# Ring of five weight slots with in-place low parts, and the order of silu, cast, product and split

## The reference

```python
def first_block(x, ...):
    proj = rmsnorm(h, norm1_w) @ w_in
    o_d = diff_attention(...)            # 8 heads, two softmax maps each
    o_c = chunk_attention(...)           # 8 heads
    merged = sigmoid(gd) * (o_d @ w_branch_diff) + sigmoid(gc) * (o_c @ w_branch_chunk)
    h = h + merged @ w_out
    h = h + peer(rmsnorm(h, norm2_w), wq, keys, u, v)   # top 16 of 128 x 128 keys, gelu(x u) * g, @ v
    return rmsnorm(h, final_norm_w)

def swiglu(x, w_gu, w_down):
    gate, up = split(x @ w_gu, 2)        # 1024 -> 2 x 2816
    return (silu(gate) * up) @ w_down

def second_block(x, ...):
    x = x + 0.5 * rms_norm(swiglu(rms_norm(x, ffn1_pre_g), ffn1_w_gu, ffn1_w_down), ffn1_post_g)
    x = x + rms_norm(hybrid_mixer(rms_norm(x, mix_pre_g), ...), mix_post_g)
    x = x + 0.5 * rms_norm(swiglu(rms_norm(x, ffn2_pre_g), ffn2_w_gu, ffn2_w_down), ffn2_post_g)
    return x
```

## Time and profile before

| | us |
|---|---|
| median of 3 runs | 1537.48 |
| lowest and highest run | 1533.52, 1541.29 |
| the profiled execution | 1530.73 |
| its span, first to last instruction | 1529.2 |
| PE busy with matmuls | 1495.4 (98%) |
| DVE busy | 1114.7 (73%) |
| ACT busy | 738.3 (48%) |
| POOL busy | 267.9 (18%) |

### The profile page before, as it was taken

One profiled execution on the slowest core, in us unless ns is written; L12 is line 12 of the kernel. 1 busy time (PEld: TensorE's weight loads), 2 busy tenths in 40 slices (PEclk: granted clock), 3 DMA queues, 4 the chain that ended last, 5 costly groups with the idle time before them and its releaser, 6 DMA issues. The chain is left out here.

```text
span 1529.2 us, 27764 instructions
## 1 busy us (share of the span) xinstructions
PE 1495.4 (98%) x10806; PEld 1378.3 (90%) x10806; DVE 1114.7 (73%) x1579; ACT 738.3 (48%) x850; POOL 267.9 (18%) x306
## 2 busy tenths in 40 slices
PE   8999999999999999999999999999899999999998
PEld 7888998999999999998888888889899888899986
DVE  5657666699999989837676777677677576777753
ACT  4366753545454455444444444445344457644431
POOL 1100000000000111025565456540000010000000
PEclk9999999999999999999999999999999999999999
DMA  6553343666665777797877778774556543255551
GB/s 250 211 193 139 118 150 105 214 245 237 235 235 207 255 234 272 259 325 286 288 287 280 298 289 299 285 257 152 190 197 212 195 143 127 97 190 196 193 200 74
DMA packets 56535, 329.47 MB, mean 215 GB/s; under 512 B 7520, under 2 KB 7568, under 8 KB 25088
## 3 DMA queue, kind: packets, MB, share of 16 engines
q1 hardware_dynamic: 36144, 259.01, 47.0%
q0 software_dynamic: 20304, 69.21, 13.1%
HBM read 294.64 MB, written 33.55 MB: 215 GB/s over the span
## 5 line engine op out<-in xcount | busy, mean ns | idle before, releaser
L954 DVE TENSOR_TENSOR wl<-raw,wh 128x2048 fp32r<-128x2048 f32 x244 | 586.9, 2406 | 257.0 <-ACT wh L552 255.8
L552 ACT CAST wh<-raw 128x2048 fp32r<-128x2048 f32 x244 | 466.2, 1911 | 400.6 <-DMA raw<-in_wstream 333.0
L1878 PE MATMUL ub<-xh,wh 128*128 128x256 f32 x2168 | 613.1, 283 | 12.7 <-DVE fg L1069 7.2
L1879 PE MATMUL ub<-xl,wh 128*128 128x256 f32 x2168 | 604.8, 279 | 0.0
L1880 PE MATMUL ub<-xh,wl 128*128 128x256 f32 x2168 | 604.8, 279 | 0.0
L1878 PEld LDWEIGHTS ub<-xh,wh 128*128 128x128 f32 x2168 | 411.5, 190 | 21.9 <-DVE fg L1069 7.8
L1879 PEld LDWEIGHTS ub<-xl,wh 128*128 128x128 f32 x2168 | 412.8, 190 | 0.1
L1880 PEld LDWEIGHTS ub<-xh,wl 128*128 128x128 f32 x2168 | 411.3, 190 | 0.0
L1878 PE MATMUL acc<-wh,ah 128*128 128x512 f32 x512 | 200.0, 391 | 0.2
L1880 PE MATMUL acc<-wh,al 128*128 128x512 f32 x512 | 199.2, 389 | 0.0
L1879 PE MATMUL acc<-wl,ah 128*128 128x512 f32 x512 | 199.2, 389 | 0.0
(11 more groups left out here) (373 smaller groups left out, 1667.4 us busy)
## 6 DMA issues: line engine op xcount, KB each, us to landing
raw<-in_wstream SPq DMA_DIRECT2D x244, 1024.0 KB, 4.9
gates<-gst POOLq DMA_DIRECT2D x16, 1024.0 KB, 15.5
gl_in<-gates POOLq DMA_DIRECT2D x64, 256.0 KB, 4.9
hidden<-hid POOLq DMA_DIRECT2D x60, 256.0 KB, 4.5
hid<-hidden POOLq DMA_DIRECT2D x60, 256.0 KB, 4.8
resid<-in_x SPq DMA_DIRECT2D x2, 512.0 KB, 3.9
raw<-in_wstream SPq DMA_DIRECT2D x2, 512.0 KB, 7.2
rb<-in_rel POOLq DMA_DIRECT2D x1, 1024.0 KB, 8.7
```

The lines of the kernel that those rows point to most:

```text
L552: act.copy(wh[:, slot, :], raw[:, slot % RAW, :]).then_inc(w_high, 1)
L954: v.tensor_tensor(wl[:, slot, :], raw[:, slot % RAW, :], wh[:, slot, :].bitcast(F32), ALU.subtract).then_inc(w_low, 1)
L1878: pe.matmul(dst, sh, mh, start=first, stop=False)
L1879: pe.matmul(dst, sh, ml, start=False, stop=False)
```

## The change

- The ring has five slots. `raw` has five as well, and it is laid in the same bytes as `wl`: a chunk lands where its low part will stand, and DVE subtracts in place. `wh` grows from four to five slots; the total of the three is what it was (80 KB per partition).
- SP loads chunk c when PE is finished with chunk c-5 (`c_done`). Five chunks are loaded at the start in place of two. ACT's cast waits for the landing alone.
- `AHEAD` stays 3.
- Loops over four chunks no longer fit a ring of five. Those of the hidden stage and of the feed-forward stages are written out; those of the value stage on ACT, DVE and PE have a body of 20 chunks (`VBODY`).
- In the feed-forward stages ACT runs the silu of a unit in front of the cast, for the written-out units as silu 0, `ahead(C + 1)`, silu 1, `ahead(C + 2)` and so on, and a silu of one column is put in front of the first one. From unit 6 on DVE runs take and finish in front of the low part. Between units 5 and 6 both engines thus have one conversion fewer, and each later one stands one unit later than before.

```diff
-RAW = 2
-RING = 4
-AHEAD = RING - 1
+RING = 5
+AHEAD = 3
+VBODY = 4 * RING
...
-        raw = sb("raw", [P, RAW, CW])
         wh = sb("wh", [P, RING, CW], F32R)
+        st = ExitStack()
+        raw = sb("raw", [P, RING, CW], at=st)
+        st.close()
         wl = sb("wl", [P, RING, CW], F32R)
...
-            sp.dma_start(raw[:, 1, :], stream[1]).then_inc(raw_in[1], 16)
-
-            def load(c, slot):
-                sp.wait_ge(w_low, c - RAW + 1)
-                sp.dma_start(raw[:, slot, :],
-                             stream[bass.ds(c, 1)].rearrange("a p n -> p (a n)")).then_inc(raw_in[slot], 16)
...
+            for c in range(1, RING):
+                sp.dma_start(raw[:, c, :], stream[c]).then_inc(raw_in[c], 16)
+
+            with sp.Fori(0, NCH // RING - 1) as i:
+                for j in range(RING):
+                    sp.wait_ge(c_done, i * RING + (j + 1))
+                    sp.dma_start(raw[:, j, :], stream[bass.ds(i * RING + (RING + j), 1)]
+                                 .rearrange("a p n -> p (a n)")).then_inc(raw_in[j], 16)
...
-                act.wait_ge(raw_in[slot % RAW], arrived(c, slot))
-                if not isinstance(c, int) or c >= RING:
-                    act.wait_ge(c_done, c - RING + 1)
-                act.copy(wh[:, slot, :], raw[:, slot % RAW, :]).then_inc(w_high, 1)
+                slot = c % RING
+                act.wait_ge(raw_in[slot], c // RING * 16 + 16)
+                act.copy(wh[:, slot, :], raw[:, slot, :]).then_inc(w_high, 1)
...
-            with act.Fori((TOPK_U + SPREAD_U) // 4, 15) as i:
-                for j in range(4):
-                    hidden_step(i * 4 + j, j)
+            for n in range(TOPK_U + SPREAD_U, 60):
+                hidden_step(n, n)
...
-            with act.Fori(0, 15) as i:
-                for j in range(4):
-                    value_step(i, j)
+            with act.Fori(0, 60 // VBODY) as i:
+                for j in range(VBODY):
+                    high_step(i * VBODY + (j + 1), j + 1)
+                    ahead_in(i, CV + j)
...
                 ahead(C)
-                ahead(C + 1)
+
+                act.activation(ssq[:, 7:8], wcol[:, 0, 0:1], ACT.Silu)
                 for j in range(6):
                     silu(U + j, nf + j, j % 2)
-                    if j >= 1 and j < 5:
+                    if j < 5:
                         ahead(C + j + 1)
-                with act.Fori(1, 5) as i:
-                    for j in range(2, 6):
-                        ahead_at(i * 4 + (C + j), C + j)
-                        silu(i * 4 + (U + j), i * 4 + (nf + j), j % 2)
+                for j in range(6, FT):
+                    silu(U + j, nf + j, j % 2)
+                    ahead(C + j)
...
-                v.tensor_tensor(wl[:, slot, :], raw[:, slot % RAW, :], wh[:, slot, :].bitcast(F32),
+                v.tensor_tensor(wl[:, slot, :], raw[:, slot, :], wh[:, slot, :].bitcast(F32),
                                 ALU.subtract).then_inc(w_low, 1)
...
-                with v.Fori(1, 5) as i:
-                    for j in range(2, 6):
-                        ahead_at(i * 4 + (C + j), C + j)
-                        take(i * 4 + (C + j), (U + j) % 2, j % 2)
-                        finish(i * 4 + (U + j), i * 4 + (nf + j), j % 2, bass.ds(i * 4 + j, 1))
+                for j in range(6, FT):
+                    take(C + j, (U + j) % 2, j % 2)
+                    finish_first(j)
+                    ahead(C + j)
...
-            with pe.Fori((TOPK_U + SPREAD_U) // 4, 16) as i:
-                for j in range(4):
-                    hidden_step(i * 4 + j, j)
+            for n in range(TOPK_U + SPREAD_U, 64):
+                hidden_step(n, n)
...
-            with pe.Fori(1, 15) as i:
-                for j in range(4):
+            with pe.Fori(1, 60 // VBODY) as i:
+                for j in range(VBODY):
                     value_step(i, j)
...
-                with pe.Fori(1, 5) as i:
-                    for j in range(2, 6):
-                        unit_chunk(i * 4 + (C + j), C + j, i * 4 + (U + j), U + j)
+                for j in range(6, FT):
+                    unit_chunk(C + j, C + j, U + j, U + j)
```

More of the change, by code:

```diff
@@ L265, in in_bank @@
             return k + 1 if k < 2 else (k | 1) + 1
-        raw_in = [sem(f"raw_in{k}") for k in range(RAW)]
+        raw_in = [sem(f"raw_in{k}") for k in range(RING)]
         first_in = sem("first_in")
@@ L546, in _, with split, ahead_in @@
         def _(act):
-            def split(c, slot):
-                act.wait_ge(raw_in[slot % RAW], arrived(c, slot))
-                if not isinstance(c, int) or c >= RING:
-                    act.wait_ge(c_done, c - RING + 1)
-                act.copy(wh[:, slot, :], raw[:, slot % RAW, :]).then_inc(w_high, 1)
-            def arrived(c, slot):
-                return ((c - slot % RAW) // RAW) * 16 + 16 if isinstance(c, int) else \
-                    (c - slot % RAW) * (16 // RAW) + 16
-            def ahead(c):
[L561 to L565, removed]
+            def split(c):
+                slot = c % RING
+                act.wait_ge(raw_in[slot], c // RING * 16 + 16)
+                act.copy(wh[:, slot, :], raw[:, slot, :]).then_inc(w_high, 1)
+            def ahead(c):
+                if c + AHEAD < NCH:
+                    split(c + AHEAD)
+            def ahead_in(i, c):
+                c += AHEAD
+                slot = c % RING
+                act.wait_ge(raw_in[slot], i * (VBODY // RING * 16) + (c // RING * 16 + 16))
+                act.copy(wh[:, slot, :], raw[:, slot, :]).then_inc(w_high, 1)
             nt = [0]
@@ L741, in hidden_step @@
             def hidden_step(n, nmod):
-                ahead_at(n + CU, CU + nmod)
+                ahead(n + CU)
                 act.wait_ge(c_done, n + (CU + 1))
@@ L791, in _ @@
                 hidden_step(n, n)
[L793 to L797, removed]
-            with act.Fori(0, 15) as i:
-                for j in range(4):
-                    value_step(i, j)
-            for j in range(4):
-                value_step(15, j)
+            with act.Fori(0, 60 // VBODY) as i:
+                for j in range(VBODY):
+                    high_step(i * VBODY + (j + 1), j + 1)
+                    ahead_in(i, CV + j)
+            for n in range(60, 64):
+                if n < 63:
+                    high_step(n + 1, n + 1)
+                    ahead(n + CV)
             def ffn(gu, dn, nf, w, stage):
@@ L959, in ahead, with ahead_in @@
                     low(c + AHEAD, (c + AHEAD) % RING)
-            def ahead_at(c, cmod):
-                low(c + AHEAD, (cmod + AHEAD) % RING)
+            def ahead_in(i, c):
+                low(i * VBODY + (c + AHEAD), (c + AHEAD) % RING)
             def guess(dst, src, ti):
@@ L1447, in _ @@
                 gates_step(1, j)
-            with v.Fori((TOPK_U + SPREAD_U) // 4, 15) as i:
-                for j in range(4):
-                    ahead_at(i * 4 + (CU + j), CU + j)
+            for n in range(TOPK_U + SPREAD_U, 60):
+                ahead(n + CU)
             def lowpart(n, k):
@@ L1459, in _ @@
                     lowpart(0, 0)
-                ahead_at(n + CU, CU + n)
-            def value_step(i, j):
-                n = i * 4 + j
-                if not (isinstance(n, int) and n == 63):
-                    lowpart(n + 1, j + 1)
-                    ahead_at(n + CV, CV + j)
-            with v.Fori(0, 15) as i:
-                for j in range(4):
-                    value_step(i, j)
-            for j in range(4):
-                value_step(15, j)
+                ahead(n + CU)
+            with v.Fori(0, 60 // VBODY) as i:
+                for j in range(VBODY):
+                    lowpart(i * VBODY + (j + 1), j + 1)
+                    ahead_in(i, CV + j)
+            for n in range(60, 64):
+                if n < 63:
+                    lowpart(n + 1, n + 1)
+                    ahead(n + CV)
             def weigh(tt):
@@ L2138, in _ @@
             pe.wait_ge(g_sb, GROUPS)
-            for j in range(4):
+            for j in range(VBODY):
                 value_step(0, j, first=j == 0)
-            with pe.Fori(1, 15) as i:
-                for j in range(4):
+            with pe.Fori(1, 60 // VBODY) as i:
+                for j in range(VBODY):
                     value_step(i, j)
             for j in range(3):
-                value_step(15, j)
+                value_step(60 // VBODY, j)
             pe.wait_ge(a_l, 64)
```

17 lines of the change are left out of this document (5 added, 12 removed).

## The result

The changed kernel takes 1509.95 us in the median of 4 runs (1506.42 to 1512.35), beside 1535.5 (1531.08 to 1541.29) for the kernel before on the same chip: ratio 0.9837, 95% interval 0.9804 to 0.987 (the ratios here are those on record; they can differ by some tenths of a per cent from the quotient of two medians). The forecast was 1523.2, its range 1515 to 1532. The direction is right. The gain is 25.6 us, where 14.3 were forecast.

What follows compares the result with a forecast made beforehand. PE was taken as busy for 1495.4 of 1529.2 us, losing 14.3 us at two feed-forward starts; 14.0 net there plus 0.3 at the first attention, 14.3 off the median 1537.48, gave 1523.2, range 1515 to 1532.

Steps and rivals of the forecast that it cites:

- In the steady state nothing moves: Loads released by PE: a chunk lands about when its cast was allowed before, so only feed-forward starts gain.
- I take the difference off the median: Forecast gain of 14.3 us, worked out on the profiled execution, subtracted from the median 1537.48 to give 1523.2.
- First feed-forward stage: PE's waits for fg and the slow clock behind them go, through earlier loads and new orders: all 6.3 us.
- Second feed-forward stage: Same chain plus a table load moved ahead by a dummy silu: 8.0 us lost, waits and slow clock to go.
- detour of the fifth chunk: Start of both feed-forward stages: its cast now stands behind silu 0; price 0.3 us for both, bounds 0 and 2 x 1.9.
- Depth of the ring: Five slots for raw and converted chunks together: cost 0, since value, the tightest stage, fits landings up to 10.1 us.
- rival A: Value stage: late landings make it slower than before, 21 us for six chunks, 1544 us; 6 in 100.
- the 0.75: Chance given to faster (under 1529.8 us): forecast, E, C and half of B put at 77, two off for spread.
- rival E: More gain: attention's wait with its slow stretch and a wait near 43 us vanish, 3 to 4 us, 1519.5; 10 in 100.
- rival C: Value stage: the long loop's jump stops PE once, up to 6.3 us, 1529.5, or some 1528; 5 in 100.
- B: Only one feed-forward stage's stall goes; the first stage's 6.3 us stay, 1529.5; 12 in 100.
- Low part in place: DVE subtracting in the same bytes: at most 0.15 us per chunk, taken as 0, bound 0 to 1 us.

Runs made afterwards that it cites:

- e4: The kernel before with its feed-forward, hidden and value loops written out, value in bodies of 20 chunks: 1534.13 us, ratio 0.9983.
- e1: The kernel before, unedited, run again: 1534.31 us, ratio 0.999.
- e2: The kernel before with only the changed kernel's orders in the feed-forward stages: 1526.93 us, ratio 0.9929.
- e3: The changed kernel with the old orders of the feed-forward stages put back: 1512.5 us, ratio 0.9834.
- e5: The changed kernel, unedited, run again: 1512.26 us, ratio 0.9856 to the kernel before.
- e6: The changed kernel with every cast also waiting until PE is done with chunk c-4: 1512.46 us, ratio 0.9858 to the kernel before.
- e8: The changed kernel with the second cast and its low part moved forward at the start of both feed-forward stages: 1507.26 us, ratio 0.9821 to the kernel before.
- e11: On top of e8, PE waits for the take of unit 5 before unit 6 in the second feed-forward stage: 1509.25 us.
- e14: On top of e8, two unused transposes in front of unit 6 of the second feed-forward stage: 1511.21 us.
- e10: On top of e8, a fourth transpose in each of the two turns of the indices (product-key stage): 1506.37 us, ratio 0.9833 to the kernel before.
- e9: The changed kernel with loads from the third chunk on also waiting for the low part two chunks back: 1528.33 us, ratio 0.9971 to the kernel before.
- e12: The kernel of e8 once more, no further edit: 1508.1 us, ratio 0.9842 to the kernel before.
- e13: On top of e8, one unused transpose in front of unit 6 of the second feed-forward stage: 1508.21 us.
- e7: The changed kernel with each load released one chunk of PE later: 1656.86 us, ratio 1.0811 to the kernel before.

## Why the prediction was wrong

**The step that failed is "In the steady state nothing moves."** It argued that a chunk requested when PE has finished c-5 lands about when the old kernel allowed its cast. That compares the new landing with the old permission to cast, and not with the old landing. The old landing came later: the load waited for the low part two chunks back, and the low part for a cast that had itself waited for its chunk, a loop that went round with hardly any slack: landing 5.7, cast 1.91 and a low part of 2.70 in the mean are 10.3 us for two chunks, for which PE takes 10.9. The 115.5 us that ACT stood in front of casts in the value stage show it. The loads say the same: before, one is issued 19.1 us in the median (17.0 to 21.2) ahead of PE's start on its chunk in value, after it 21.4 each time. Because the loop had so little slack, disturbances reached PE: near 42 us, in the attention, in front of the gates, in value. In value they didn't come through late weights, whose low part was ready at least 6 us early, but through the hidden tile's split, which is queued on ACT behind the cast that waits. Third unit, attention, gates, last hidden units and value together, in us:

```
ring of four      before 717.6   e4 719.2   e1 720.1   e2 720.8
ring of five      711.9 to 712.5 in nine profiles (after, e3, e5, e6, e8, e11 to e14;
                  e10, with its wait at the gates, 713.4)
with old release  e9 728.4
```

The forecast had 0.3 us for all of that. The ring gives 5.5 against the profile of before and 7 to 9 against those of e4, e1 and e2, and e9 brings the waits back by the old release alone. The other 2.6 of the 8.1 us stand at the start, and no run ties them to the release.

**A second step failed with it: "I take the difference off the median."** The waits of the steady state vary between executions: by the sums above the profiled execution of before had 1.6 to 3.2 us fewer of them than those of e4, e1 and e2, and it lay 5 to 7 us under its median. The changed kernel has these waits no more; its own runs, 6 us apart, vary at least by PE's two paces. So the medians are 25.6 apart and the profiles 18.7. That is the larger part of the miss: of the 13.3 us between forecast and median, 4.4 are the profiles' (18.7 against 14.3), 6.9 this step, and 2.0 that the kernel before has a median of 1535.5 in four runs and not 1537.48. Of a change that removes a source of scatter the median gives back more than the fast execution shows.

**First feed-forward stage: right.** Forecast 6.3 us, measured 6.0. The casts find their chunks, the granted clock stays at 1.00, and from unit 6 on the takes come in time. That the orders do this, though, is only half true: e3 has the old orders and no stall in this stage. DVE's 3.15 us of idle time in front of unit 5's product stay with the orders alone and go with the ring alone. DVE in e2 and then in e3, where it still makes both low parts in front of the take:

```profile
1093.37 0.43 DVE L1557 TENSOR_TENSOR ff<-fs,fg 128x256 f32<-128x256 f32 x1 [3.33 <-issue]
```

```profile
1077.95 0.42 DVE L1545 TENSOR_TENSOR ff<-fs,fg 128x256 f32<-128x256 f32 x1
...
1080.52 4.49 DVE L946 TENSOR_TENSOR wl<-raw,wh 128x2048 fp32r<-128x2048 f32 x2
```

The late chunk was the stall; the order alone only moves one low part out of its way.

**Second feed-forward stage: mechanism right, size wrong.** Forecast 8.0 (less some detour), measured 4.6. The stalls and the slow clock went. In their place the stage ran from its fifth unit on at the slower of two paces at full clock. The window of the kernel after, as in e14:

```profile
1360.00:1420.00 60.00, 60.00 (x512) 1.00 0.57 193
```

At 532 it would have taken 120.3 us, as e8, e10 and e12 do, so this took back 3.9 us, a term that the forecast hadn't. The detour of the fifth chunk cost little by itself: PE slips by 0.05 and 0.08 us at the fifth unit, in front of which the low part ends just in time. Whether that slip sets the slow pace stays open. For it: without the slip (e8, e10, e12) both stages were fast in three profiles of three, and the runs of each lie within 2 us; e11 and e13, which have no slip there either, are fast too. Against it: e6 has the same slip and a fast stage, the first stage of after has the 0.07 us slip and stays fast, e3's first stage turns slow at the ninth unit with no slip over 0.02 us, and e11's wait of 0.95 us does nothing.

**Depth of the ring: the value was right, the reason wrong.** Cost 0, as forecast, and rival A did not come. But the margin of 10.1 us was worked out wrongly and in the wrong stage. It gave landing, cast and low parts three periods of PE, 16.3 us, where the release at c-5 leaves four (21.4 us in the trace, so 15.2 for a landing); and what runs out first is ACT's arrival at the cast, after 5.8 us. e7 shows that one chunk less of it costs 147 us by its medians (1656.86 against 1509.95, or 145 against e5), half of it in the attention, where ACT has urgent work behind each cast. The chance of 6 in 100 for A rested on landings of value alone. That the forecast of no cost held is thus in part luck. The sum behind the 0.75 is off as well: forecast, E, C and half of B are 81 in 100, and not 77.

**Low part in place, unrolling, jumps: right, all 0.** The low part takes 2.29 us as before where GpSimd is idle. In the value stage it even became shorter in the mean. DVE's group there (760 to 1040), before and after:

```profile
L954 DVE TENSOR_TENSOR wl<-raw,wh 128x2048 fp32r<-128x2048 f32 x52 | 140.3, 2697 | 79.8 <-ACT wh L552 79.8
L1454 DVE TENSOR_TENSOR al<-hid,ah 128x512 fp32r<-128x512 f32 x51 | 60.4, 1184 | 2.9 <-ACT ah L786 2.9
```

```profile
L947 DVE TENSOR_TENSOR wl<-raw,wh 128x2048 fp32r<-128x2048 f32 x50 | 120.7, 2415 | 56.3 <-ACT wh L562 52.9 <-ACT wh L550 3.4
L1447 DVE TENSOR_TENSOR al<-hid,ah 128x512 fp32r<-128x512 f32 x50 | 36.9, 737 | 58.5 <-ACT ah L782 58.5
```

The mean fell from 2.70 to 2.42 us and that of the hidden tile's low part from 1.18 to 0.74: they are the same instructions, likely at other times beside GpSimd's products, whose own mean rose from 1.87 to 2.31 us. Over the whole kernel that is 18 and 29 us less, which covers DVE's 42 us. It touches the end only through the slack that it gives the chain, and no run separates it. For rival C, the jump: e4 has the body of 20 chunks and costs nothing, and in the kernel after no chunk of value begins late. The Trainium skill's page "Runtime: NRT & Kernel Launch" (Instruction fetch mechanics) gives PE a store of 128 KiB, or 2048 instructions, in which such a body fits by an estimate (20 x 48 = 960 matmuls and weight loads); the trace agrees, with 82 instruction packets in all and no stop.

**Attention and start: rival E, at its price.** The attention gives 2.0 us: its wait at the first softmax goes from 1.5 to 1.1, and the 3.6 us at clock 0.53 that followed it are gone. Before:

```profile
98.70:102.30 3.60, 3.60 (x20) 3.60 (x19) 2.39 (x8) 0.88 (x4) 0.00 (x0) 0.53 0.31 75
```

The wait near 43 us gives 1.1. Rival E had this at 3 to 4 us in all and was right on its places. The start gave 2.6 us where up to 2 lost had been feared; the first weight matmul comes at 10.2 to 11.9 us in the four profiles of the ring of four and at 10.0 to 10.2 in the twelve of the ring of five, e9 among them, and none of the runs separates the ring's part in it. With rival E added the forecast would have been 1519.5, still 9.6 over the median.

## What to carry to other kernels

Read what the conversion engines wait for in the steady state before calling it quiet: 2 us in front of every cast for its landing is a loop almost without slack where the load's release itself hangs on those conversions, even if PE shows no long wait, and the scatter of the runs is its sign. Where PE releases the load, such a wait can be harmless: in the last stage of the kernel after (1450 to 1529) the casts wait 3.1 us each for their landings and PE never does. Release a load so that no recent conversion has to be done first, and count its time not up to the consumer's need but up to the place where an in-order engine will stand and wait for it with other work behind. Two edits that cure the same stall needn't add; try each alone before crediting either.

## What the runs showed of the hardware

PE runs pairs of weight load and 256-column matmul at 0.1134 or at 0.118 us each with the granted clock at 1.00 in both (532 or 512 in 60 us), for tens of microseconds on end. Small things ahead of a stretch can decide which: three transposes went with a change of pace in the stage of the product keys in 14 profiles of 14, four did not in one; in the second feed-forward stage two brought the slow pace (one profile, and by their times all six runs), one did not. But the same kernel without any edit had its first feed-forward stage fast in one profile and slow in another (after and e5), so that instructions alone don't decide it, and no run here gives the rule. It is 4% of the time of such a stretch, in a kernel whose PE is busy 99% of it. The 512-column matmuls had one pace in all 16 profiles (0.227 in the value stage).
